# Seven half-size products in place of eight in a transformer block's output projection, and layer-norm statistics from a running total behind its expert blocks

## What is computed

```python
y_ssd = ssd_output(y_f, y_b, xs, z, p)                  # 1024 tokens x 1024
o = gqa_block_attention(q, k, v)                        # 1024 tokens x 1024
mix = jnp.concatenate([y_ssd, o], -1) @ p['w_out']      # (1024 x 2048) @ (2048 x 1024)
x = layer_norm(alpha * x + g_a * mix, ln1_g, ln1_b)
x = layer_norm(alpha * x + g_f * hier_moe(x * (1 + sc_f) + sh_f, p), ln2_g, ln2_b)
```

## Time and profile before

| | us |
|---|---|
| median of 3 runs | 3162.27 |
| lowest, highest | 3158.41, 3162.52 |
| the profiled execution | 3158.29 |
| its span in the trace | 3156.3 |
| PE busy | 2967.4 (94%) |
| DVE busy | 1485.7 (47%) |
| ACT busy | 733.8 (23%) |
| POOL busy | 1074.8 (34%) |
| L1484, the output projection | 256 products in 512 passes, from 1341.0 to 1575 |

### The profile page before, as it was taken

How to read it: one execution, slowest core, us unless ns; L and a number is a source line. 1 busy time by engine, 2 the same in 40 slices (tenths; PEclk the granted TensorE clock), 3 DMA queues, 4 the chain that set the end, 5 groups by cost and what they waited for, 6 DMA issues and landing times.

```text
span 3156.3 us, 28771 instructions
## 1 busy us (share of the span) xinstructions
PE 2967.4 (94%) x10259; PEld 1481.1 (47%) x10259; DVE 1485.7 (47%) x2421; ACT 733.8 (23%) x1543; POOL 1074.8 (34%) x971
## 2 busy tenths in 40 slices
PE   8998999999899999999969993998999999999999
PEld 4554554444455555444434441566444444444443
DVE  2434883345666666422254425545132444444446
ACT  2223855411133333301011112323110000000002
POOL 0002870000267677700022002832022455555542
PEclk8999999999899999999969996999999999999999
DMA  7001322000100000020078887003020111121101
GB/s 271 20 0 47 93 82 97 27 27 1 54 1 1 1 1 1 11 75 30 27 251 317 356 352 219 24 0 120 0 80 27 40 40 40 40 67 53 40 14 60
DMA packets 130686, 237.52 MB, mean 75 GB/s; under 512 B 25544, under 2 KB 81520, under 8 KB 120688
## 3 DMA queue, kind: packets, MB, share of 16 engines
q1 hardware_dynamic: 120016, 206.11, 18.4%
q0 software_dynamic: 5760, 16.78, 1.8%
q10 hardware_dynamic: 4768, 12.79, 1.1%
HBM read 235.65 MB, written 26.22 MB: 83 GB/s over the span
## 4 chain that ended last, share of the span: by engine, by line
PE 81%; DVE 5%; issue 3%; DMA 1%; ACT 1%; POOL 1%; DVEq 0%; SPq 0%; POOLq 0%; ACTq 0%
PE ps L3254 17%; PE ps L3270 8%; PE ps L1484 7%; PE ps L1077 6%; PE ps L2017 5%; PE ps L1254 5%; PE ps L1273 4%; PE ps L1289 4%; PE ps L3006 4%; PE ps L988 3%; PE ps L2038 3%; PE ps L2277 2%; PE ps L887 1%; PE ps L2975 1%; PE ps L1279 1%
## 5 line engine op out<-in xcount | busy, mean ns | idle before, releaser
L1366 DVE TENSOR_REDUCE arena_b<-ps 128x1 f32<-128x512 f32 (+1 forms) x384 | 217.5, 599 | 149.4 <-PE ps L1254 149.1
L3379 DVE TENSOR_TENSOR arena_d<-arena_d,ps 128x512 f32<-128x512 f32 x154 | 101.8, 684 | 388.3 <-PE ps L3254 388.3
L3219 POOL TENSOR_TENSOR arena_b<-arena_b,arena_d 128x512 f32<-128x512 f32 x120 | 150.7, 1269 | 362.8 <-DVE arena_d L3401 361.5
L1348 POOL TENSOR_TENSOR arena_b<-arena_b 128x512 f32<-128x512 f32 x182 | 224.6, 1269 | 97.4 <-ACT arena_b L1330 97.4
L1254 PE MATMUL ps<-arena_d,arena_a 64*128 64x512 f32 (+1 forms) x768 | 240.1, 552 | 3.7 <-DVE arena_b L1357 2.9
L1273 PE MATMUL ps<-arena_a,arena_d 64*128 64x512 f32 x640 | 220.0, 607 | 2.4 <-ACT arena_b L1330 1.8
L3398 DVE TENSOR_TENSOR arena_b<-arena_b,ps 128x512 f32<-128x512 f32 x240 | 158.8, 685 | 32.8 <-POOL arena_b L3219 23.6
L1077 PE MATMUL ps<-ring,arena_b 128*128 128x512 f32 x384 | 167.4, 592 | 0.0
L564 PE MATMUL ps<-arena_b,ring 128*128 128x512 f32 x384 | 167.1, 593 | 0.0
L1330 ACT ACTIVATE arena_b<-ps 128x512 f32<-128x512 f32 x214 | 116.1, 595 | 212.8 <-PE ps L1279 212.8
L3254 PE MATMUL ps<-arena_a,ring 128*128 128x512 f32 x352 | 155.3, 600 | 2.8 <-DMA ring<-in_w_up 2.8
(11 more groups left out here) (580 smaller groups left out, 5343.6 us busy)
## 6 DMA issues: line engine op xcount, KB each, us to landing
ring<-in_w_gate SPq DMA_DIRECT2D x33, 1024.0 KB
ring<-in_w_up SPq DMA_DIRECT2D x33, 1024.0 KB
ring<-in_w_down SPq DMA_DIRECT2D x33, 1024.0 KB
ring<-in_w_in SPq DMA_DIRECT2D x10, 2048.0 KB, 9.5
ring<-in_w_mod SPq DMA_DIRECT2D x32, 512.0 KB, 3.9
yslots<-arena_a ACTq DMA_DIRECT2D x24, 512.0 KB, 4.3
arena_d<-in_w_gate SPq DMA_DIRECT2D x10, 1024.0 KB
arena_d<-in_w_up SPq DMA_DIRECT2D x10, 1024.0 KB
```

What stands on the lines that cost most here:

```text
L1348: eng.tensor_tensor(acc, first, prT[n % NPR], ALU.add).then_inc(s_pa, 1)
L1366: eng.tensor_reduce(mx3[j % 2][:, t, e, piece:piece + 1], ps[:, shared("s", u), 0:k1 - k0], AX.X, ALU.max).then_inc(s_mx, 1)
```

## The change

Output projection. Tokens are split into a lower half (tiles 0 to 3) and an upper one (4 to 7), columns of `w_out` into two halves, and the inner dimension into `mixl` and `mixu`. The eight products of quarters are replaced by seven (Strassen's scheme in Winograd's form), each of 4 token tiles by 8 products. What they need are four sums of left quarters (s1 to s4) and four of right quarters (t1 to t4), each a `tensor_tensor` of 128 x 4096 on VectorE, written over quarters that are no longer needed. Each product's PSUM result is added on VectorE into the one or two places of `x1` where it belongs; where it belongs in both column halves it is read twice through a broadcast access. `OUT_ORDER` gives the order of the products, `OUT_STEPS` that of VectorE's steps, and one semaphore, `s_wot`, counts them. The stage's first three token tiles wait for attention's last exponential where all waited for its end; their banks are 3, 4 and 5. The gate row is made behind the first product. The DMA of x follows the new order of the half tiles.

Stage x2. The sum of the two parts is a `scalar_tensor_tensor` that also puts out the row's total. A `tensor_scalar` makes minus the mean of it, ScalarE the sum of squared deviations (Square with a bias and an accumulator) and its root, with the division by 1024 and epsilon inside. The two `bn_stats`, `bn_aggr` and the epsilon step go. The norm of tile 0 stands before the sum of tile 1. On ScalarE the 16 gains of `w_in_2` stand ahead of the whole stage, and the copy of a turned tile ahead of the sum of squares.

```diff
+        OUT_HALVES = [(t, 0) for t in range(4)] + [(t, 1) for t in range(4, LT)] + \
+            [(t, 1) for t in range(4)] + [(t, 0) for t in range(4, LT)]
+        OUT_ORDER = ["p1", "p2", "p7", "p5", "p6", "p3", "p4"]
+        OUT_STEPS = [("p1", t) for t in range(4)] + ["s3", "s1", ("p2", 0), ("gated", 0), "t1", ("p2", 1), ("gated", 1),
+                                                     "t3", ("p2", 2), ("gated", 2), ("p2", 3), ("gated", 3)]
...
+        OUT_SUMS = {"p7": "t3", "p5": "t1", "p6": "t2", "p3": "s4", "p4": "t4"}
+
+        def out_made(what):
+            return OUT_STEPS.index(what) + 1
+
+        def out_bank(u):
+            return ps[:, 3 + u if u < 3 else u % 3, :]
+
+        mlo, mhi = mixl[:, :, 0:HALF], mixl[:, :, HALF:]
+        ulo, uhi = mixu[:, :, 0:HALF], mixu[:, :, HALF:]
+        b11, b21, b12, b22 = slot(J_OUT), slot(J_OUT + 1), slot(J_OUT + 2), wo4
+        OUT_OPERANDS = {"p1": (mlo, b11), "p2": (ulo, b21), "p7": (mlo, b12), "p5": (mhi, b11), "p6": (mlo, b12),
+                        "p3": (ulo, b22), "p4": (uhi, b11)}
...
-            for u in range(2 * LT):
-                t, n = u // 2, u % 2
-                if n == 1 and t >= 3:
-                    store(t - 3)
-                if u >= 4:
-                    eng.wait_ge(s_wod, u - 3)
-                eng.dma_start(xl[u % 4], io["x"][0, t * P:(t + 1) * P, n * HALF:(n + 1) * HALF]
-                              ).then_inc(s_xl[u % 4], 16)
-            for t in range(LT - 3, LT):
+            for i in range(2 * LT):
+                t, n = OUT_HALVES[i]
+                if i >= 4:
+                    eng.wait_ge(s_wod, i - 3)
+                eng.dma_start(xl[i % 4], io["x"][0, t * P:(t + 1) * P, n * HALF:(n + 1) * HALF]
+                              ).then_inc(s_xl[i % 4], 16)
+                if i >= 12:
+                    store(i - 12)
+            for t in range(4, LT):
...
+            after(eng, "mod2")
+            eng.wait_ge(s_ex, 20 * NJOB)
+            wait_panel(eng, J_OUT)
+            for i, name in enumerate(OUT_ORDER):
+                left, right = OUT_OPERANDS[name]
+                for t in range(4):
+                    u = 4 * i + t
+                    if u == 3:
+                        after(eng, "att")
+                    if u == 4:
+                        pe_row(eng, 2, 0)
+                        wait_panel(eng, J_OUT + 1)
+                    if t == 0 and name in OUT_SUMS:
+                        eng.wait_ge(s_wot, out_made(OUT_SUMS[name]))
+                    if name == "p3" and t == 0:
+                        eng.wait_ge(s_rope, 32 + 48)
+                    if u >= 6:
+                        eng.wait_ge(s_wot, out_made((OUT_ORDER[(u - 3) // 4], (u - 3) % 4)))
+                    for k in range(KT):
+                        mm = eng.matmul(out_bank(u), left[:, k, t * P:(t + 1) * P], right[:, k, :],
+                                        start=(k == 0), stop=(k == KT - 1))
+                    mm.then_inc(s_wo, 1)
+                    r = u - 20
+                    if r >= 1:
+                        if r == 1:
+                            eng.wait_ge(s_rgc, 1)
+                        pe_turn_tile(eng, r - 1, x1[:, r - 1, :], lambda t: eng.wait_ge(s_l1, N_L1 * (t + 1)), 0)
+                    if r >= 2:
+                        pe_logits(eng, r - 2)
+            pe_turn_tile(eng, LT - 1, x1[:, LT - 1, :], lambda t: eng.wait_ge(s_l1, N_L1 * (t + 1)), 0)
...
+            def added(name, t, dst, op=ALU.add):
+                out_step(eng.tensor_tensor(dst, dst, product(name, t), op), (name, t))
+
+            def summed(name, dst, a, b, op):
+                out_step(eng.tensor_tensor(dst, a, b, op), name)
+
+            def finished(i):
+                t, n = OUT_HALVES[i]
+                cs = upper if n else lower
+                out_step(eng.tensor_tensor(x1[:, t, cs], x1[:, t, cs], rowg[:, cs], ALU.mult), ("gated", i))
+                eng.wait_ge(s_xl[i % 4], 16 * (i // 4 + 1 + N_XL[i % 4]))
+                step(eng, eng.scalar_tensor_tensor(out=x1[:, t, cs], in0=xl[i % 4], scalar=ALPHA,
+                                                   in1=x1[:, t, cs], op0=ALU.mult, op1=ALU.add),
+                     s_wod, i + 1)
+                ins = eng.bn_stats(bst[:, t, n, :], x1[:, t, cs])
+                if i >= 8:
+                    ch = Chain(eng, s_lv, N_LV * t)
+                    ch(ins)
+                    ch(eng.bn_aggr(mv[:, t, :], bst[:, t, :, :].rearrange("p a b -> p (a b)")))
+                    ch(eng.tensor_scalar(mv[:, t, 1:2], mv[:, t, 1:2], EPS_LN, None, ALU.add))
+                    dve_norm(eng, 0, t)
+
+            after(eng, "att")
+            for t in range(4):
+                p1 = product("p1", t)
+                eng.tensor_copy(both(t), bc(p1, 1, 2))
+                out_step(eng.tensor_copy(both(t + 4), bc(p1, 1, 2)), ("p1", t))
             row_copy(eng, 0)
...
+            wait_panel(eng, J_OUT)
+            wait_panel(eng, J_OUT + 2)
+            eng.wait_ge(s_rope, 32 + 48)
+            summed("s3", mlo, mlo, mhi, ALU.subtract)
+            summed("s1", mhi, mhi, uhi, ALU.add)
+            for t in range(4):
+                added("p2", t, x1[:, t, lower])
+                finished(t)
+                if t == 0:
+                    summed("t1", b11, b12, b11, ALU.subtract)
+                if t == 1:
+                    summed("t3", b12, b22, b12, ALU.subtract)
+            for t in range(4):
+                out_step(eng.tensor_tensor(both(t + 4), both(t + 4), bc(product("p7", t), 1, 2), ALU.add), ("p7", t))
+            summed("s2", mlo, uhi, mlo, ALU.subtract)
+            for t in range(4):
+                pair = x1[:, t:LT:4, upper]
+                out_step(eng.tensor_tensor(pair, pair, bc(product("p5", t), 1, 2), ALU.add), ("p5", t))
+                if t == 0:
+                    summed("t2", b12, b22, b11, ALU.subtract)
+            summed("s4", ulo, ulo, mlo, ALU.subtract)
+            wait_panel(eng, J_OUT + 1)
+            for t in range(4):
+                p6 = product("p6", t)
+                eng.tensor_tensor(x1[:, t, upper], x1[:, t, upper], p6, ALU.add)
+                out_step(eng.tensor_tensor(both(t + 4), both(t + 4), bc(p6, 1, 2), ALU.add), ("p6", t))
+                finished(t + 4)
+                if t == 0:
+                    summed("t4", b11, b12, b21, ALU.subtract)
+            for t in range(4):
+                added("p3", t, x1[:, t, upper])
+                finished(t + 8)
+            for t in range(4):
+                added("p4", t, x1[:, t + 4, lower], ALU.subtract)
+                finished(t + 12)
...
+            for i in range(2 * KT):
+                act_gains(eng, i // KT, i % KT)
+
+            def squares(u):
+                eng.wait_ge(s_l1, N_L1 * (LT + u + 1))
+                eng.wait_ge(s_silu, x2_squared(min(u + 1, LT - 1) if u else 0))
+                if u:
+                    eng.wait_ge(s_ssq, u)
+                eng.activation(sqj, x1[:, u, :], ACT.Square, accum_out=ss8[:, 0, u:u + 1]).then_inc(s_ssq, 1)
+
             for t in range(LT + 3):
+                if t == 1:
+                    squares(0)
                 if t < LT:
-                    act_norm(eng, 1, t)
+                    eng.wait_ge(s_lv, N_LV * LT + t + 1)
+                    if t:
+                        eng.wait_ge(s_ssq, max(t - 1, 1))
+                        eng.wait_ge(s_silu, x2_squared(t - 1))
+                    eng.activation(sqj, x1[:, t, :], ACT.Square, bias=mv[:, t, 0:1], accum_out=mv[:, t, 1:2]
+                                   ).then_inc(s_silu, 1)
+                    eng.wait_ge(s_silu, x2_squared(t))
+                    eng.activation(rs8[:, t:t + 1], mv[:, t, 1:2], ACT.Sqrt, scale=1.0 / D, bias=epsln
+                                   ).then_inc(s_silu, 1)
+                if t >= 3:
+                    u = t - 3
+                    eng.wait_ge(s_hmT, LT + u + 1)
+                    eng.copy(hn[:, :, u * P:(u + 1) * P], turned(u)).then_inc(s_hm, 1)
                 if 2 <= t < LT + 2:
                     u = t - 2
                     eng.wait_ge(s_rv, 2 * u + 1)
                     eng.activation(rr8[:, 0, u:u + 1], ss8[:, 0, u:u + 1], ACT.Sqrt).then_inc(s_ra, 1)
...
-                    for i in (2 * u, 2 * u + 1):
-                        act_gains(eng, i // KT, i % KT)
...
-                    step(eng, eng.tensor_tensor(x1[:, t, :], x1[:, t, :], g1[t % 4], ALU.add), s_gx, LT + t + 1)
-                    dve_stats(eng, 1, t)
+                    step(eng, eng.scalar_tensor_tensor(out=x1[:, t, :], in0=x1[:, t, :], scalar=1.0, in1=g1[t % 4],
+                                                       op0=ALU.mult, op1=ALU.add, accum_out=mv[:, t, 0:1]),
+                         s_gx, LT + t + 1)
+                    step(eng, eng.tensor_scalar(mv[:, t, 0:1], mv[:, t, 0:1], -1.0 / D, None, ALU.mult),
+                         s_lv, N_LV * LT + t + 1)
                 if t >= 2:
```

(6 more changed lines are left out.)

88 lines of the change are left out of this document (35 added, 53 removed).

## The result

The changed kernel takes 3117.92 us, the median of 4 runs (3116.29 to 3118.64); the kernel before took 3160.34 beside it. The ratio is 0.9868, 95% interval [0.9851, 0.9885], so 1.3% less time. The profiled execution takes 3118.30, 40.0 less than that of before; I had said 38.7 less, and a median of 3121.5.

What follows compares the result with a forecast made beforehand. TensorE, busy 94%, was taken to bound the kernel, VectorE stage x2. Projection 30.9 and x2 7.8 us, together 38.7, off 3158.3 gave 3119.6 profiled, median 3121.5; range 3114 to 3134, chance 0.72.

Steps and rivals of the forecast that it cites:

- The units and the start: Output projection, TensorE: 28 units of 6.87 us, 192.4 in place of 219.8, the first starting at about 1333.6.
- The gate row keeps its 3.4 us: Output projection, TensorE: the gate row, moved behind unit 3, was to cost 3.4 us as before.
- The tail: End of the output projection: the last tile has one more VectorE operation of 512 columns, costing 0.7 us.
- t3: Output projection: VectorE's sum t3 done at 1389.5, wanted by TensorE at 1392.0; 2.5 us early, the stage's tightest place.
- Rival 1: Output projection: VectorE holds TensorE at p7; at 6.5 per sum 5.7 us are lost, time 3127; chance 0.12.
- Rival 2: Stage x2: the total makes the sum stream its columns twice, 1.06 more; x2 gives 0.8, time 3128.5; chance 0.12.
- ScalarE 4.8: it fits below 4.93: Stage x2: ScalarE's work per tile, 4.8 us, fits within the new step of 4.93, before 6.24.
- The start of x2: Stage x2: root's table load adds 1.28 on the path; tile 2's sum starts at about 1941.03, before at 1942.16.
- Sum: Whole kernel: 30.9 us from the output projection and 7.8 from stage x2, 38.7 less for the profiled execution.
- The median: Timed runs: median put at 3121.5, halfway, since two of three earlier runs lay 4 above the profiled execution.
- Rival 4: No change: TensorE waits for a norm at every turn in p3 and p4, about 5 us at each of seven; chance 0.02.
- Rival 3: Slower than before: each of four sums before p7 takes over 14.8 us; at 17 the time is about 3169; chance 0.02.

Runs made afterwards that it cites:

- the extra sums: Changed kernel with one or three more 128x4096 VectorE operations ahead of t3: TensorE stalls 2.71 and 11.63 us, row sums to last turn 219.1 and 229.7.
- the late copy: Changed kernel with ScalarE's copy of a turned tile in x2 moved behind the next scaling: 3116.45 us, ratio 0.9869.
- the last edits: Changed kernel with ScalarE's copy moved, filler between x2 turns, both, both plus filler ahead of the projection's last turn: 3116.45, 3113.48, 3116.55, 3111.50 us.

## Why the prediction was right, and where it was not

- *The units and the start.* 6.87 a unit, 28 of them, no gap; unit 0 at 1333.36 (said: 1333.6). Right.
- *"The gate row keeps its 3.4 us".* Mis-sized: 1.78. The row of before showed its price behind 4.19 us of idle time, and I carried it to a place with none. This is most of the 1.8 by which the last unit ended earlier than said (1541.70, said 1543.5).
- *The tail.* One more operation was to cost 0.7; turn behind turn is 6.77 against 5.97, 0.8. Right. Projection: 32.6, said 30.9.
- *t3.* Sum 4.42 and step 4.46 (said 4.41 and 4.45), done 1388.53, wanted 1390.18. It has 1.65 in hand, not 2.5, since TensorE came 1.8 earlier than I had it and VectorE only 1.0. The tightest place was named rightly, and the extra sums priced it. That the gate row's new place is what gives VectorE this time I had not seen.
- *Rival 1.* Not met, and its upper price was built wrongly: I doubled the 3.23 of rows 5 to 6.5, as if GpSimd made an operation longer in proportion. What GpSimd cost in these traces is a wait of up to one of its operations, not a factor. Even with GpSimd at work all the time, TensorE lost 0.45.
- *The sum with a total.* 1.23 + 0.08; said 1.28 + 0.19. Rival 2 fell: there is no second pass over the columns, though both sources are f32 in SBUF.
- *"ScalarE 4.8: it fits below 4.93".* The step that failed. The sum of ScalarE's work was nearly right (5.25 - 0.60 = 4.65), but it doesn't run unbroken: its copy waits 0.60 for TensorE's turn, which takes 1.97 at a granted clock of 0.50 and waits for ScalarE's own scaling. Step 5.25; the late copy alone brings 4.7. I had added up each engine and not followed the loop through both.
- *The start of x2.* The table load stands on the path, as said (1901.51, 1.28). Tile 2's sum starts 8.7 behind the first, said 9.5, which pays back most of the slow steps: up to the turn of tile 4 x2 gave 7.4, said 7.8. That this is so near is partly luck, two misses of opposite sign.
- *End.* 40.5 at the first quarter (32.6, 7.4, 0.4 of the gains, and 0.2 in the expert blocks), 40.0 in the time. In between the two traces lie 38.1 to 40.4 apart, so no one place took the 0.5. TensorE waits 3.6 us for a panel in the feed-forward where it waited 2.8, but only because the turn ahead of it took 1.09 and not 1.97; from that turn's start to the panel it is 4.67 and 4.76.
- *Sum.* 38.7 said, 40.0 measured in the profiled execution; + 1.7 for the projection and - 0.4 for x2 are what the stages show.
- *The median.* Said 3121.5, measured 3117.92. Of these 3.6 us 1.3 are the sum; 2.3 are the offset, which I took over from the kernel before: there the median lay above the profiled execution, here it lies 0.4 below.
- *Rival 4*, turns that wait in p3 and p4: not met, none of these turns names a wait. *Rival 3*, slower than before, would need over 40 us more on VectorE ahead of t3; three whole extra sums cost 13.6.

## What to carry to other kernels

The price of an instruction on TensorE belongs to the place where it was read: behind 4.19 us of idle time it was nearly twice what it is in the middle of work, so moving one into work gained more than the stall. It also gave the engine beside it time to get ahead. Where two engines hand a tile back and forth, follow one tile once around through both, with its waits; that each engine's own sum fits into the step says little. And when work is to move to an engine with room, look for the first result that somebody waits for: its slack (here 1.65 us) is the price of the whole stage, not the engine's share of 50 or 60%.

## What the runs showed of the hardware

- A sum of 128x4096 in place costs 4.42 whether or not TensorE reads the same arenas (s3 on arena_c alone, s1 and t1 on arenas that p2 reads), and a scalar_tensor_tensor of 1024 f32 columns with a total 1.23 and a read of 0.08.
- VectorE and GpSimd wait for each other by whole operations where both read two tensors from SBUF (a GpSimd product of 0.73 took 5.01 beside a sum of 4.42; VectorE's operations of 0.69 took 1.10 and 1.18).
- Filler of 2.6 us between the turns, with gaps of 1.1 to 1.5 left, held the granted clock at 1.00 and turns at 1.09; without it they stood at 0.50 and 1.97. At the later wait half clock followed in two of the three traces with 3.2 to 3.3 us of idle time, and in one of the eleven with 2.2 to 2.3.
- In 800 to 900, far ahead of any edit, the granted clock was 0.87 to 0.96, and with it the time to attention's end moved by up to 7.8 us from one execution to the next. That is more than any of the last edits gains, and why they are judged by their traces.
